# Two expert layers with gated outputs kept as two rounded halves, a one-hot combination, and nine extra homes for weight panels

## The reference, cut to what matters

```python
def ec_moe(h, w_router, w_gate, w_up, w_down):     # h: (1, 512, 1024); 16 experts, 1024 wide
    cap = max(1, EC_FACTOR * n // N_EXPERTS)        # 64 tokens for each expert
    aff = jax.nn.softmax(h @ w_router, axis=-1)
    gate, idx = lax.top_k(swapaxes(aff, 1, 2), cap) # each expert chooses its 64 tokens
    xs = h[idx]
    a = silu(xs @ w_gate) * (xs @ w_up)
    out = (a @ w_down) * gate[..., None]
    return zeros.at[idx].add(out)                   # summed back by token
x = x + m_lat[..., 5, :] * ec_moe(...)
```

## Time and profile before

| | |
|---|---|
| median of three runs | 3340.39 us |
| the profiled execution's own time | 3338.58 us |
| its span, first to last instruction | 3336.8 us |
| TensorE busy | 3025.6 us (91%) |
| VectorE, ScalarE busy | 1112.0, 877.3 us |
| mean granted clock of TensorE | 0.955 |
| bytes read | 632.48 MB |

### The profile page before, as it was taken

One profiled execution on the slowest core, in us unless ns is written; L12 is line 12 of the kernel. 1 busy time (PEld: TensorE's weight loads), 2 busy tenths in 40 slices (PEclk: granted clock), 3 DMA queues, 4 the chain that ended last, 5 costly groups with the idle time before them and its releaser, 6 DMA issues.

```text
span 3336.8 us, 41503 instructions
## 1 busy us (share of the span) xinstructions
PE 3025.6 (91%) x18502; PEld 2036.5 (61%) x18502; DVE 1112.0 (33%) x1572; ACT 877.3 (26%) x1320; POOL 0.2 (0%) x4
## 2 busy tenths in 40 slices
PE   6997899999997899999899988889999976999998
PEld 3775778888765777888677667554433353443443
DVE  3446632242536543223343347420000136000002
ACT  3443232232544233223433531311000032010001
POOL 0000000000000000000000000000000000000000
PEclk9998999999998899999899999889999997999999
DMA  7224323223233222222552041379999932999996
GB/s 267 78 99 152 103 76 98 92 95 95 79 116 148 68 89 89 92 92 95 177 163 74 13 192 62 106 294 409 409 408 409 401 133 101 364 409 409 408 409 268
DMA packets 247442, 637.27 MB, mean 191 GB/s; under 512 B 12896, under 2 KB 110176, under 8 KB 247136
## 3 DMA queue, kind: packets, MB, share of 16 engines
q1 hardware_dynamic: 244128, 627.22, 50.6%
q10 hardware_dynamic: 3136, 7.40, 0.6%
HBM read 632.48 MB, written 2.10 MB: 190 GB/s over the span
## 4 chain that ended last, share of the span: by engine, by line
PE 72%; DVE 8%; DMA 6%; ACT 5%; PEld 4%; issue 3%; PEldq 1%; SPq 1%; ACTq 0%; DVEq 0%
PE ps L612 69%; PEld ps L612 4%; DMA ring<-in_w_exp_gate 3%; PE ps L626 3%; ACT h L1580 1%; PEldq L1083 1%; DMA proj<-in_w_exp_gate 1%; ACT mix_halves L1583 1%; DMA ring<-in_w_exp_up 1%; DMA ring<-in_ada_w 1%; SPq L600 1%; ACT proj L1997 0%; DMA ring<-in_w_mod 0%; DVE work L2288 0%; DVE work L2881 0%
## 5 line engine op out<-in xcount | busy, mean ns | idle before, releaser
L612 PE MATMUL ps<-mix_halves,work_halves 128*128 128x512 f32 (+1 forms) x1544 | 622.1, 403 | 44.4 <-DVE h_halves L2139 34.4
L612 PE MATMUL ps<-h_halves,work_halves 128*128 128x512 f32 (+1 forms) x1544 | 608.9, 394 | 4.8 <-ACTq L1494 2.4
L612 PE MATMUL ps<-mix_halves,ring_halves 128*128 128x512 f32 x1448 | 568.3, 392 | 0.0
L2139 DVE TENSOR_TENSOR ring_halves<-ring,work_halves 128x2048 fp32r<-128x2048 f32 (+2 forms) x125 | 252.6, 2021 | 550.4 <-ACT work_halves L1503 453.9
L612 PE MATMUL ps<-ring,work 128*64 128x512 f32 x1680 | 389.1, 594 | 20.9 <-DMA ring<-in_w_exp_gate 18.2
L612 PEld LDWEIGHTS ps<-mix_halves,work_halves 128*128 128x128 f32 (+1 forms) x1544 | 290.8, 188 | 130.9 <-issue 48.8
L612 PEld LDWEIGHTS ps<-h_halves,work_halves 128*128 128x128 f32 (+1 forms) x1544 | 291.7, 189 | 72.6 <-issue 6.4
L612 PEld LDWEIGHTS ps<-mix_halves,ring_halves 128*128 128x128 f32 x1448 | 272.6, 188 | 60.8
L612 PEld LDWEIGHTS ps<-ring,work 128*64 128x64 f32 x1680 | 128.0, 137 | 254.6 <-issue 254.3
L2539 DVE SCALAR_TENSOR_TENSOR x<-ps,small,x 128x512 f32<-128x512 f32 x112 | 82.3, 750 | 598.5 <-PE ps L612 597.0
L1503 ACT ACTIVATE work_halves<-ring 128x2048 fp32r<-128x2048 f32 x102 | 188.2, 1845 | 337.2 <-PE ps L612 336.1
(11 more groups left out here) (377 smaller groups left out, 3318.1 us busy)
## 6 DMA issues: line engine op xcount, KB each, us to landing
ring<-in_w_exp_gate SPq DMA_DIRECT2D x114, 1024.0 KB, 11.3
ring<-in_w_exp_down SPq DMA_DIRECT2D x100, 1024.0 KB, 13.0
ring<-in_w_exp_up SPq DMA_DIRECT2D x96, 1024.0 KB, 15.2
ring<-in_ada_w SPq DMA_DIRECT2D x48, 1024.0 KB, 7.1
ring<-in_w_mod SPq DMA_DIRECT2D x48, 1024.0 KB, 7.5
proj<-in_w_exp_up SPq DMA_DIRECT2D x28, 1024.0 KB, 12.8
proj<-in_w_exp_down SPq DMA_DIRECT2D x28, 1024.0 KB, 15.9
ring<-in_w_in SPq DMA_DIRECT2D x22, 1024.0 KB, 5.3
```

The costliest lines, as they stand in the source:

```text
L612: i = pe.matmul(o, lhsT, rhs, start=start, stop=stop, **kw)
L2139: to("lo", tt(rounded(v), v, rounded(hi), ALU.subtract))
```

## The change

- The homes are nine instead of six: two of `proj` until pair 2; two more of `proj`, a two-piece one beside `e_actT`, the two of `h` and one in `work` for pair 0 only; and one in `stage_tables` for all pairs. The two later homes of `proj`, until pairs 4 and 6, are gone, since the outputs' lower halves lie there.
- TensorE multiplies the selection with the affinities (`slot_gates`: 32 float32 matmuls with 128 columns of weights and 16 moving ones) between gate and up of pair 0, and VectorE picks each slot's gate out of the result. The gated selection `r_pg` is gone.
- ScalarE copies the output of a pair gated and rounded (`y_hi`), VectorE writes what is left (`y_lo`); the selection itself is turned. A combination is now two fp32r matmuls instead of one float32 matmul.
- The order inside a pair: of two tiles to be turned, one is turned after gate and one after up; the blocks of a combination stand after gate, after the gather and after the transposes; the copies of the transposes to SBUF go in two halves, and down begins with the first.
- The down panels of pair 7 are cut by columns (128 x 4 x 512 instead of 128 x 2 x 1024), so that half the output's columns are done after four of eight panels, and half the combination is done before the last two.

```diff
-SPARE = (("y", 0, 0), ("y", 2048, 2), ("y", 4096, 4), ("y", 6144, 6), ("h", 0, 0), ("h", 2048, 0))
+SPARE = (("y", 2048, 2), ("y", 6144, 2), ("y", 0, 0), ("y", 4096, 0), ("act", 8192, 0), ("h", 0, 0), ("h", 2048, 0),
+         ("gates", 5120, 0), ("tables", 0, 7))
...
+                            if e == E - 2 and w == "w_exp_down":
+                                v = a[w][l, e + s, j % 2 * 512:j % 2 * 512 + 512, j // 2 * 512:j // 2 * 512 + 512]
+                                panels.append((v.rearrange("(k p) n -> p k n", p=P), 4, 512))
+                                continue
...
-                     5: (range(3, 5), range(0, 4)), 6: (range(3, 5), range(4, 8)), 7: (range(5, 7), range(0, 4))}
+                     5: (range(3, 5), range(0, 4)), 6: (range(3, 5), range(4, 8)), 7: (range(5, 7), range(0, 8))}
...
+                    if where == "h":
+                        sp.wait_ge(sem["r_tok_sb"], 8 * (l + 1))
+                    elif where == "gates":
+                        sp.wait_ge(sem["r_thr"], l + 1)
+                    else:
                         sp.wait_ge(sem["r_logits"], l + 1)
...
+                def slot_gates():
+
+                    for p in range(8):
+                        for n in range(NT):
+                            mm(ps[:, 6, p * E:p * E + E], sel[:, n, p * P:p * P + P], r_aff[:, n, :],
+                               n == 0, n == NT - 1, "r_slots" if p == 7 and n == NT - 1 else None)
...
                 def combine(pairs, m, bank):
 
+                    claim(bank)
                     for p in pairs:
-                        mm(ps[:, bank, :], y_store[:, p, m * P:m * P + P], r_pgT[:, p, :], p == pairs[0], p == pairs[-1],
+                        s = slice(m * P, m * P + P)
+                        mm(ps[:, bank, :], rounded(y_hi[:, p % 4, s]), rounded(selT[:, p, :]), p == pairs[0], False)
+                        mm(ps[:, bank, :], rounded(y_lo[:, p % 4, s]), rounded(selT[:, p, :]), False, p == pairs[-1],
                            "down" if p == pairs[-1] else None)
...
                 for p in range(8):
-                    pair(0, x_sel, "e_gate", (0, 2))
+                    pair(0, x_sel, "e_gate", (0, 2), "x_sel_sb")
                     if p == 0:
                         pe.wait_ge(*due("r_marks"))
-                    turn_gates(gate_tiles.get(p, ()))
+                        slot_gates()
                     if p:
-                        pe.wait_ge(*due("y_sb"))
-                    if p in combining:
-                        combine_blocks(*combining[p])
+                        pe.wait_ge(*due("y_lo"))
+                    if p in gate_tiles:
+                        turn_selection(gate_tiles[p][0], 6)
+                    sources, blocks = combining.get(p, ((), ()))
+                    for m in blocks[:2]:
+                        combine(sources, m, 6 + m % 2)
+                    for bank in (2, 3):
+                        claim(bank)
                     pair(2, x_sel, "e_up")
...
+                    for m in blocks[2:-2]:
+                        combine(sources, m, 6 + m % 2)
                     pe.wait_ge(*due("e_act"))
                     for k in range(KB):
-                        turn(ps[:, k // 4, k % 4 * P:k % 4 * P + P], e_act[:, k * P:k * P + P], "aT" if k == KB - 1 else None)
-                    pe.wait_ge(*due("aT_sb"))
-                    pair(4, e_actT, "e_down")
...
+                        turn(ps[:, k // 4, k % 4 * P:k % 4 * P + P], e_act[:, k * P:k * P + P], "aT" if k % 4 == 3 else None)
+                    for m in blocks[-2:]:
+                        combine(sources, m, 2 + m % 2)
...
+                    if p < 7:
+                        pair(4, e_actT, "e_down", (0, 2), "aT_sb")
+                for half in range(2):
+                    for j in range(2):
+                        if half == 0:
+                            pe.wait_ge(*due("aT_sb"))
+                        if half and j:
+                            pe.wait_ge(*due("y_lo"))
+                            for m in range(4):
+                                combine(last_pairs, m, m)
+                        w = [panel(), panel()]
+                        for k in range(4 * j, 4 * j + 4):
+                            for e in range(2):
+                                s = slice(e * 64, e * 64 + 64)
+                                mm(ps[s, 4 + half, :], e_actT[:, k, s], w[e][:, k % 4, :],
+                                   k == 0, k == KB - 1, "e_down" if k == KB - 1 and e else None)
+                        free[0] += 2
+                pe.wait_ge(*due("y_lo"))
+                for m in range(4, KB):
                     combine(last_pairs, m, m)
...
-                    to("y_sb", f(y_store[:, p, :], ps[:, 4:6, :].rearrange("p b f -> p (b f)"), ACT.Copy))
+                        to("y_sb", f(rounded(y_hi[:, p % 4, :]), ps[:, 4:6, :].rearrange("p b f -> p (b f)"), ACT.Copy,
+                                     scale=r_gates[:, p:p + 1]))
...
+                    to("y_lo", stt(out=rounded(y_lo[:, p % 4, s]), in0=ps[:, banks, :].rearrange("p b f -> p (b f)"),
+                                   scalar=r_gates[:, p:p + 1], in1=rounded(y_hi[:, p % 4, s]),
+                                   op0=ALU.mult, op1=ALU.subtract))
```

More of the change, by code:

```diff
@@ L276 @@
     "r_thr_rows": "TensorE: on all partitions", "r_thr_sb": "ScalarE: in SBUF", "r_marks": "VectorE: marks to be counted",
-    "r_count": "TensorE: their running counts", "r_pg": "VectorE: a tile's gates by slot", "r_pgT": "TensorE: turned",
-    "r_pgT_sb": "ScalarE: in SBUF", "x_sel": "TensorE: a pair's tokens", "x_sel_sb": "ScalarE: in SBUF",
+    "r_count": "TensorE: their running counts", "r_slots": "TensorE: affinities of a slot's token",
+    "r_gates": "VectorE: a slot's gate", "selT": "TensorE: a tile's selection, turned", "selT_sb": "ScalarE: in SBUF", "x_sel": "TensorE: a pair's tokens", "x_sel_sb": "ScalarE: in SBUF",
     "e_gate": "TensorE: a pair's gates", "e_up": "TensorE: its ups", "e_exp": "ScalarE: silu(gate)",
     "e_act": "VectorE: silu(gate) up", "aT": "TensorE: turned", "aT_sb": "ScalarE: in SBUF",
-    "e_down": "TensorE: a pair's output", "y_sb": "ScalarE: in SBUF", "pooled": "VectorE: a pooled group",
+    "e_down": "TensorE: a pair's output", "y_sb": "ScalarE: gated, upper halves", "y_lo": "VectorE: lower halves", "pooled": "VectorE: a pooled group",
 }
@@ L531, in slot @@
                 where, start, _ = SPARE[seat[n] - RING]
-                return cut(proj_all if where == "y" else hflat, start, k * width, k=k, n=width)
+                if where == "act":
+                    whole = proj_all[:, start:start + width]
+                    return bass.AP(tensor=whole.tensor, offset=whole.offset, ap=[whole.ap[0], [2048, k], [1, width]])
+                return cut({"y": proj_all, "h": hflat, "gates": work, "tables": stage_tables}[where], start, k * width, k=k, n=width)
             return cut(ring, seat[n] * PANEL, k * width, k=k, n=width)
@@ new lines, in experts @@
+                for p in range(8):
+                    if p == 0:
+                        dve.wait_ge(*due("r_slots"))
+                        for r, own in ((slice(0, 64), 0), (slice(64, P), 1)):
+                            i = dve.tensor_copy(r_gates[r, :], ps[r, 6, own:own + 127:18])
+                        to("r_gates", i)
+                    else:
+                        lower_output(p - 1, slice(4, 6), slice(0, D))
+                    blocks = combining.get(p, ((), ()))[1]
+                    for m in blocks[:2]:
+                        add(gate, m, 6 + m % 2, "down", "down_x")
@@ L2860, in experts @@
                     dve.wait_ge(*due("e_exp"))
-                    if p in combining:
-                        for m in combining[p][1]:
-                            add(gate, m, 6 + m % 2, "down", "down_x")
                     dve.wait_ge(*due("e_up"))
                     to("e_act", tt(e_act, e_tmp, ps[:, 2:4, :].rearrange("p b f -> p (b f)"), ALU.mult))
-                for m in range(4, KB):
-                    add(gate, m, 6 + m % 2, "down", "down_x")
+                    for m in blocks[2:-2]:
+                        add(gate, m, 6 + m % 2, "down", "down_x")
@@ L2869, in pooling @@
+                    for m in blocks[-2:]:
+                        add(gate, m, 2 + m % 2, "down", "down_x")
+                dve.wait_ge(*due("r_gates"))
+                for half in range(2):
+                    lower_output(7, slice(4 + half, 5 + half), slice(half * 512, half * 512 + 512))
+                    for m in range(4 * half, 4 * half + 4):
+                        add(gate, m, m, "down", "down_x")
             def pooling():
```

96 lines of the change are left out of this document (47 added, 49 removed).

## The result

The changed kernel takes 3354.69 us (median of 4 runs, 3352.40 to 3356.35), the kernel before, on the same chip, 3338.79 us (4 runs, 3334.97 to 3344.84). The ratio is 1.0051, with a 95% interval of 1.0032 to 1.0069: slower. The forecast of 3345 was 9.7 us short, and the time lies 1.7 us above the range. For the change itself +4.4 us was forecast and +15.9 measured: the kernel before took 1.6 us less this time than the 3340.39 that the forecast started from.

A forecast was written before the change was run, and what follows sets the result against it. Transfers were taken to bound each expert layer until its last panel lands, then a tail. Per layer 7.0 + 1.2 less 5.6 or 6.4 gave +2.6 and +1.8, so 3340.4 + 4.4, said as 3345 us; range 3331 to 3353.

The forecast's parts named there:

- the price of `slot_gates`: Between gate and up of pair 0: 64 instructions at 0.107 us, 6.8 us (to 7.3), delaying down and a seat's release.
- rival 1: TensorE's clock falls during `slot_gates`, so up begins at 1.2 GHz: 1.6 us a spell, 3348 us in all; 35% likely.
- rival 3: `slot_gates` costs only 1.6 us, each layer 5.2 us shorter than forecast, 3334 us; 5% likely.
- Homes: Early panels bring nothing: SP waits before panel 27 for pair 0's down; panel 28 lands 7.0 us later a layer.
- where 6.1 was forecast: Later start of pair 0's down: 6.8 us for `slot_gates` less 0.7 us gained at the transposes' copy.
- Transposes: Down starts 1.3 to 1.5 us after the transposes' start instead of 2.15; 1.5 taken, a gain of 0.7 us.
- Panels of 512 columns: Last eight panels of a layer have half-length runs, 8 x 0.15 = +1.2 us; bounds 0 and 3.2 us.
- The tail: From last panel's landing to the sums' end: 14.7 us instead of 20.3 and 21.1, gains of 5.6 and 6.4 us.
- the 0.6 ahead of the last group: In the tail, TensorE's work from up's end comes out about 0.6 us after the last panel's landing.
- From down on the forecast was -3.5: First layer after pair 0's down: rest of the +7.0 beyond down's 6.1, +1.2 for 512-column panels, -5.6 for the tail.
- the 6.5 of the first layer: Before the change, panel 28 is issued at 2241.0 and lands 6.5 us later, at 2247.5; the base for +7.0.
- The upper bounds of the prediction's own terms: Range's upper side: `slot_gates` +1.0, 512-wide panels +4.0, a transfer stutter of 1.5 us in each layer; 3351 us.

The follow-up runs named there:

- Run 5: Changed kernel with the 16 affinities repeated four times, 64 moving columns in `slot_gates`, gates still right: 3344.34 us, ratio 1.0029 to the kernel before.
- run 2: Changed kernel with 64 moving columns instead of 16 in `slot_gates`, same place, gates then wrong: 3343.17 us, ratio 1.0017 to the kernel before.
- run 10: Changed kernel with `slot_gates` in four groups of eight, one behind each quarter of pair 0's down, 16 columns: 3333.62 us, ratio 0.9991 to the kernel before.
- run 9: Changed kernel with pair 7 whole again: 128x2x1024 down panels, one 1024-column copy, all eight blocks after it: 3356.79 us, ratio 1.0058 to the kernel before.
- run 1: Changed kernel with the same 32 `slot_gates` matmuls moved behind pair 0's down: 3341.94 us, ratio 1.0018 to the kernel before.
- runs 3: Changed kernel without the two pair-0 homes `act` and `gates`: 3354.29 us, ratio 1.0046 to the kernel before.
- run 4: Changed kernel with the `stage_tables` home first and a pair-0 home of `proj` last: 3349.81 us, ratio 1.0034 to the kernel before.

## Why the prediction was wrong

**The step that failed** is the price of `slot_gates`, "64 x 0.107 = 6.8 us (to 7.3)", with nothing in the sum for the clock. It measured 8.73 and 9.26 us, and up behind it was 1.84 and 2.99 us longer than its 13.84: together 3.8 and 5.4 us more than the 6.8.

Most of this is the clock. Run 5 has the same work at 2.4 GHz and reaches the gather 35.05 us after the first gate matmul, the changed kernel 38.29 and 39.97: the low clock cost 3.2 and 4.9 us. The prediction had this as rival 1 at 35%, so the fall of the clock was seen. But it priced a spell at 1.6 us, from a spell of 3.2 us; here one spell a layer lasts 6.8 and 10.2 us, over the end of `slot_gates` and the start of up. What it set against the rival, that weight loads run all through `slot_gates`, did not hold the clock: PEld is busy all the time from 2218 to 2219, where the clock falls. That the narrow run brings the clock down is shown: 64 columns in its place keep 2.4 GHz and bring the stretches from 488.8 and 490.4 to 485.5 and 485.4 (run 5; run 2 likewise), and so do 16 columns in groups of eight between groups of 512 columns (run 10).

A smaller part, 0.5 us, has nothing to do with the clock: at 2.4 GHz the run costs 0.114 (64 columns) to 0.118 us an instruction, nearer to the gather's 0.113 than to the 0.107 I took, so 7.3 us. The moving columns don't set that pace, as forecast, since four times as many cost nothing; that the weights do fits every row, but no run changed the weights. The Trainium skill, TensorE: Matmul & The Clock Gate, section Back-to-back issue gap, gives about 25 ns for 1 to 64 moving columns, and says of its gaps that they are those of single matmuls, and that in a stream the weight loads count too. By the 25 ns alone the run would take 1.6 us; these rows contradict that use of it, and rival 3 with it.

**Homes.** Right but for the short stop at 2227.71. Panels 24 to 26 came early and counted for nothing; SP stood before `stage_tables` until 4.5 us after down began (2245.64 to 2250.17); the panel landed 5.1 us later. Down was 9.9 us later from the first gate matmul than before (46.88 against 37.02), where 6.1 was forecast: 8.73 + 1.84 - 0.81 = 9.8.

**Transposes.** 1.34 us from their start to down, where 1.3 to 1.5 was said and 1.5 taken.

**Panels of 512 columns.** The last eight landed 2.71 us apart, 0.15 over 2.56: the +1.2 us is right for the landing. As a cost it is not, since TensorE and not the last panel set the end, and run 9 got nothing back for it.

**The tail.** 15.7 us after the last landing in the first layer, where 14.7 was forecast: a gain of 4.6 instead of 5.6. In the second, the landing at 3326.2 and the sums' end at 3341.9 give 15.7 too, a gain of 5.4 instead of 6.4. The term that was off is the 0.6 ahead of the last group, which began 2680.31 - 2678.9 = 1.4 us after the landing; eight matmuls of combination took 2.0 us, not 1.8, four times over in the chain from up's end. (The prediction's "six groups of panels" in this chain are six panels, three groups; with three its 0.6 comes out.) The gated copy takes 0.69 us, not 0.65, the rest is signals. About half of this gain is of the halves: whole again, pair 7 lost 2.3 us in each layer (run 9).

**Sum again, with the measured terms.** First layer: 9.86 us later down, 2.50 us less from there on, +7.36. Second: 11.54 and 2.38, +9.16. Ahead of down 6.1 was forecast, so 3.8 and 5.4 us were missing, the price of `slot_gates`. From down on the forecast was -3.5 (0.9 + 1.2 - 5.6) and -4.3, so 1.0 and 1.9 were missing: 1.0 in each is the tail. Of the other 0.9 of the second layer, 0.7 is that the kernel before had its panel 28 sooner there, 5.8 us after the issue and not the 6.5 of the first layer, which the forecast took for both; 0.2 stays unexplained. The parts between the layers and ahead of them are 1.1 us shorter, and this gives the 15.4 of the span. The upper bounds of the prediction's own terms, added straight, give 3352.8 and not 3351; the clock was in none of them.

What I did not settle: why the low spell has two lengths (6.8 and 10.2 us, which bring the gather to 38.3 or 40.0 us after the first gate matmul, for the same instructions), and why behind dense work (run 1) the run took 10.6 and 11.5 us. It is not the layer: runs 3 and 9, with `slot_gates` as in the change, have the shorter spell in both layers, run 4 has the longer one in the second, as the changed kernel.

## What to carry to other kernels

Price a small run of matmuls with few moving columns twice: by its own instructions, and by what the clock does to it and to the dense work behind it. If it must be there, put it where nothing waits, and pad the moving side or cut the run in pieces between dense groups; here that turned +0.5% into -0.1%. More seats for early transfers are worth nothing while the queue stands before the first panel whose seat is not free: count from that panel, not from the number of homes.

## What the runs showed of the hardware beyond this

- 32 float32 matmuls of 128 x 128 weights took 7.3 us with 64 moving columns in one run, and 4 x 1.9 = 7.6 with 16 in four groups, both at full clock; with 16 in one run they took 8.7 to 11.5 us.
- A panel of 1 MB in a stream takes 2.56 us with rows of 4 KB and 2.71 with rows of 2 KB; with the 256-wide panels of the next stage it is 3.0.
- Profiled executions of kernels that are alike up to there began the first expert layer between 2192.0 and 2205.8 us. A stretch inside the layer repeats to within a microsecond or two, and from pair 0's down on to within 0.3 us (441.6 to 441.9 in ten layers), and so shows differences that the medians leave open.
